# An earlier start for the expert stage's second half: four blocks fewer before it, other gather due times, and two input loads on another DMA queue

## The reference, cut to what matters

```python
s1, s2 = q1 @ keys1.T, q2 @ keys2.T            # per head, 128 keys each
v1, i1 = top_k(s1, 16); v2, i2 = top_k(s2, 16)
top_v, top_i = top_k(v1[:, None] + v2[None, :], 16)
ids = e1 * 128 + e2; w = softmax(top_v)         # 8 heads x 16 = 128 picks a token
act = einsum('td,tkd->tk', h, u[ids])
out = einsum('tk,tkd->td', w * gelu(act), v[ids])
```

## Time and profile before

| | |
|---|---|
| median of 3 runs | 1645.26 us |
| profiled execution | 1646.56 us |
| its span in the trace | 1644.8 us |
| TensorE busy | 1535.6 us (93%) |
| VectorE busy | 1245.2 us (76%) |
| ScalarE busy | 575.4 us (35%) |
| GpSimd busy | 412.1 us (25%) |
| mean DMA rate | 263 GB/s |

### The profile page before, as it was taken

One profiled execution on the slowest core, in us unless ns is written; L12 is line 12 of the kernel. 1 busy time (PEld: TensorE's weight loads), 2 busy tenths in 40 slices (PEclk: granted clock), 3 DMA queues, 4 the chain that ended last, 5 costly groups with the idle time before them and its releaser, 6 DMA issues.

```text
span 1644.8 us, 21695 instructions
## 1 busy us (share of the span) xinstructions
PE 1535.6 (93%) x8105; PEld 1342.2 (82%) x8105; DVE 1245.2 (76%) x2343; ACT 575.4 (35%) x842; POOL 412.1 (25%) x330
## 2 busy tenths in 40 slices
PE   6899987859999899899999999969999999999997
PEld 1588877647899788899999998968888888888886
DVE  1775256764779999799999975638888888888884
ACT  3322150342223233344444443323433333333332
POOL 0000000010026677733222223314222222222211
PEclk9899897989999999999999999989999999999999
DMA  8386110311336777779999999979999998999971
GB/s 351 127 308 243 39 51 1 103 39 52 128 105 205 236 259 259 242 252 356 369 369 367 365 365 395 352 288 400 401 338 367 359 348 331 350 376 340 350 272 65
DMA packets 147829, 432.61 MB, mean 263 GB/s; under 512 B 13232, under 2 KB 46384, under 8 KB 144560
## 3 DMA queue, kind: packets, MB, share of 16 engines
q1 hardware_dynamic: 76896, 221.28, 36.8%
q0 software_dynamic: 36864, 134.23, 23.1%
q10 hardware_dynamic: 34000, 76.29, 12.2%
HBM read 377.22 MB, written 54.53 MB: 263 GB/s over the span
## 4 chain that ended last, share of the span: by engine, by line
PE 60%; DVE 12%; DMA 2%; issue 1%; ACT 1%; POOL 0%; ACTq 0%
PE ps L1547 19%; PE ps L1548 19%; PE ps L1549 19%; PE ps L1872 3%; DVE rows L1355 2%; DVE ps L1387 1%; DMA blk_raw<-u_t 1%; DMA g_dram<-g_buf 1%; DVE ps L1391 1%; DVE picks L1393 1%; PE ps L1824 1%; DVE tv L1322 1%; DVE tv L1325 1%; DVE ti L1323 1%; DVE ti L1326 1%
## 5 line engine op out<-in xcount | busy, mean ns | idle before, releaser
L1547 PE MATMUL ps<-hT_hi,ws_hi 128*128 128x384 f32 (+1 forms) x1184 | 417.0, 352 | 34.6 <-POOL ws_lo L562 16.7
L1548 PE MATMUL ps<-hT_lo,ws_hi 128*128 128x384 f32 (+1 forms) x1184 | 409.1, 346 | 0.0
L1549 PE MATMUL ps<-hT_hi,ws_lo 128*128 128x384 f32 (+1 forms) x1184 | 408.8, 345 | 0.0
L1547 PE MATMUL ps<-vs_hi,coef_hi 128*128 128x512 f32 x768 | 299.8, 390 | 3.9 <-DVE coef_lo L1521 3.9
L1548 PE MATMUL ps<-vs_lo,coef_hi 128*128 128x512 f32 x768 | 299.7, 390 | 0.0
L1549 PE MATMUL ps<-vs_hi,coef_lo 128*128 128x512 f32 x768 | 299.6, 390 | 0.0
L1547 PEld LDWEIGHTS ps<-hT_hi,ws_hi 128*128 128x128 f32 x1184 | 225.6, 191 | 47.4 <-issue 19.5
L824 ACT ACTIVATE ws_hi<-blk_raw 128x1024 fp32r<-128x1024 f32 x128 | 135.7, 1060 | 349.1 <-PE ps L1549 326.4
L888 ACT ACTIVATE vs_hi<-blk_raw 128x1024 fp32r<-128x1024 f32 x128 | 135.7, 1060 | 311.7 <-PE ps L1549 302.5
L570 POOL DMA_INDIRECT rows<-v_nat,ids x128 | 137.5, 1074 | 396.1 <-DVE ps L1472 374.0
L1518 DVE TENSOR_TENSOR vs_lo<-blk_raw,vs_hi 128x1024 fp32r<-128x1024 f32 x128 | 156.8, 1225 | 102.3 <-ACT vs_hi L888 101.5
(11 more groups left out here) (284 smaller groups left out, 1855.1 us busy)
## 6 DMA issues: line engine op xcount, KB each, us to landing
blk_raw<-u_t SPq DMA_DIRECT2D x128, 512.0 KB
blk_raw<-v_nat SPq DMA_DIRECT2D x128, 512.0 KB
g_dram<-g_buf ACTq DMA_DIRECT2D x128, 192.0 KB
w_dram<-w_stage SPq DMA_DIRECT2D x48, 512.0 KB
grp_g<-g_dram ACTq DMA_DIRECT2D x16, 1536.0 KB
grp_w<-w_dram ACTq DMA_DIRECT2D x16, 1536.0 KB
part_w<-w_ada SPq DMA_DIRECT2D x32, 512.0 KB, 6.0
raw<-w_in SPq DMA_DIRECT2D x20, 512.0 KB, 7.0
```

The lines of the kernel that those rows point to most:

```text
L1547: pe.matmul(o, lh, rh, start=start, stop=False, skip_group_check=True)
L1548: pe.matmul(o, lh, rl, start=False, stop=False, skip_group_check=True)
L1549: return pe.matmul(o, ll, rh, start=False, stop=stop, skip_group_check=True)
```

## The change

`PART_A` goes from 46 to 42, which moves `EXP_AT` from 42 to 38, `REST_DVE` from 48 to 44 and `PART_END` from 100 to 96. `EARLY_ROWS` goes from 6 to 4. A block without a spread takes no row (before three), and the blocks from 96 to 121 take the difference: 52 rows in 26 blocks, before 32 rows in 22. The blocks 122 to 127 take two v rows each, before one. The gathers' due times start earlier: the first at block 7 instead of 10, and row k of the search is expected to be used at block 10 + 23k/20 instead of 14 + 9k/8. At the start, `xs` and `cx` are loaded by ScalarE's queue behind `colp`, instead of by SP's ahead of `ada_w`.

```diff
-PART_A = 46
+PART_A = 42
 EXP_AT = PART_A - 4
 REST_DVE = PART_A + 2
-EARLY_ROWS = 6
+EARLY_ROWS = 4
@@ act_rows
     if b < PART_END:
-        return 3 if spreads_after(b) is None else 1
-    late = PICKS - EARLY_BLOCKS * SEARCH_ROWS - EARLY_ROWS - STEPS - 3 * (PART_END - PART_A - STEPS)
+        return 0 if spreads_after(b) is None else 1
+    late = PICKS - EARLY_BLOCKS * SEARCH_ROWS - EARLY_ROWS - STEPS
@@ mix_rows
     if b < EB:
-        return 1
-    late = PICKS - (EB - MIX_FROM)
+        return 2
+    late = PICKS - 2 * (EB - MIX_FROM)
@@ gathers_at
-    used = [14 + 9 * k // 8 for k in range(EARLY_BLOCKS * SEARCH_ROWS)] + [PART_A - 3] * EARLY_ROWS
+    used = [10 + 23 * k // 20 for k in range(EARLY_BLOCKS * SEARCH_ROWS)] + [PART_A - 3] * EARLY_ROWS
-    first = [used[k - G_RING] + 2 if k >= G_RING else 10 + k for k in range(PICKS)]
+    first = [used[k - G_RING] + 2 if k >= G_RING else 7 + k for k in range(PICKS)]
@@ SP's queue
-            sp.dma_start(xs[:], x.rearrange("(b p) d -> p b d", p=P)).then_inc(x_in, 16)
-            sp.dma_start(cx[:], ctxt.rearrange("(b p) d -> p b d", p=P)).then_inc(cx_in, 16)
@@ ScalarE's queue
             act.dma_start(colp[:], cols).then_inc(cols_in, 16)
+            act.dma_start(xs[:], x.rearrange("(b p) d -> p b d", p=P)).then_inc(x_in, 16)
+            act.dma_start(cx[:], ctxt.rearrange("(b p) d -> p b d", p=P)).then_inc(cx_in, 16)
             act.dma_start(ident[:], ident_in).then_inc(ident_ld, 16)
```

## The result

The changed kernel took 1662.08 us (median of 4 runs, 1658.83 to 1663.66), the kernel before 1644.28 beside it (4 runs, 1642.31 to 1646.56): ratio 1.0105 [1.0084, 1.0127], slower. The forecast was 1648.0 and its range ended at 1659. The profiled execution of after took 1661.87 us with a span of 1660.1, 15.3 us more than before; by the medians it is 17.8, since the profiled execution of before was its longest run. I account for the 15.3. The first gelu, ScalarE's in block 0, marks the start of the expert stage.

What follows compares the result with a forecast made beforehand. Bounds: TensorE in both long stages, VectorE's search between 549 and 697 us, the DMA briefly behind the spreads. Terms -4.3 - 11.5 + 16.6 + 1.9 = +2.7 us gave 1648.0 us on the median, range 1637 to 1659.

Steps and rivals of the forecast that it cites:

- The start: Program start: with tokens and ada_w in two queues, the transposes begin at 26.8 instead of 31.12 us, -4.3 us.
- two queues with work each get half: Loads at the start: each of the two queues gets 209 of the 418 GB/s.
- My bound of 0: Program start: the worst case of the -4.3 us term, late tokens eating the whole gain.
- Rival C: Program start: the queues serve the tokens first, giving -1 instead of -4.3 us, time 1651.3; chance 0.07.
- The spreads' begin: End of the search: the part with spreads begins at 685.3 instead of 696.83 us, -11.5 us.
- the stop of 10 us: Search: TensorE stands still in front of block 13 for about 10 us, waiting for row 0.
- Rival D: Search: earlier due times bring no row earlier, -7.6 instead of -11.5 us, time 1651.9; chance 0.10.
- Four blocks: Behind the spreads' begin: 86 blocks left instead of 82, at 4.16 us each, +16.6 us.
- DMA in blocks 96 to 121: End of the u half: two rows a block at 418 GB/s make a block 4.235 us, +1.9 us over 26 blocks.
- waiting beside the stores: Behind the last spread: eight stores delay one block by 7.00 us, taken as unchanged.
- rival B: End of the u half: gathered rows come late and hold up VectorE, +8.6 instead of +1.9 us, time 1654.7; chance 0.16.
- Blocks 122 to 127: End of the u half: six added v rows, 3.1 MB, taken as 0, with 7.5 us more if nothing hides them.

Runs made afterwards that it cites:

- e1: The kernel before with only the loads of xs and cx moved to ScalarE's queue behind colp: 1651.03 us against 1642.77, ratio 1.0059.
- e3: The changed kernel with one v row instead of two in each of blocks 122 to 127: 1657.67 us, ratio 1.009 to the kernel before.
- e8: The kernel before with the first ada_w piece ahead of xs and cx in SP's queue: 1642.38 us, ratio 0.9987.
- e4: The changed kernel with the u and v rows per block of the kernel before: 1655.23 us, ratio 1.0076 to the kernel before.
- e7: The changed kernel with the v half's first group load in ten pieces in blocks 110 to 120: 1654.52 us, ratio 1.0062 to the kernel before.

## Why the prediction was wrong

**The start, -4.3: wrong in sign, +5.5 at the transposes and +2.9 at the first gelu.** The step that failed is "two queues with work each get half". Measured, `ada_w` got 2.4 times the bytes of `xs`, and with pieces of equal size 1.2 times; so `xs` was used at 21.23 us instead of the 13.7 of the sum, and `cx` at 28.31 instead of 18.6. My bound of 0 was wrong as well. I had taken it that late tokens could eat no more than the gain, but TensorE had nothing else to do while they were late, and it came back at half the clock. Rival C named the right doubt, with a price of -1, and its argument that tokens go first was the wrong way round. The Trainium skill's rule that issuing from several engines saves only the time to issue ("DMA: Bandwidth & Descriptors", "Issuing engines are not separate DMA queues") would have given the same -1. That is nearer to the measured loss than my -4.3, but e1, with its loss of 8 us in the medians, shows that a second queue also changes who is served.

**The spreads' begin, -11.5: right, -10.8.** Row 23 gained 4.1 (3.9 forecast) from the two short L1395. TensorE continued behind the copies of the picks and not behind GpSimd, as forecast. Two details differ: the stop of 10 us came in two parts, and the wait behind the transposes' start was 2.9 us, not 3.6. Rival D, by which VectorE gains nothing, is out. What I didn't see is that the same rows also price the due times alone (+6.5): that the term is negative at all is owed to the four blocks moved behind it.

**Four blocks, +16.6: right** as far as it can be told apart from the next term; the part with spreads is right, 40.1 us per eight blocks.

**DMA in blocks 96 to 121, +1.9: right in sum, +2.3, by luck.** The rate was 417 GB/s as forecast, but the spacing behind the stores was 4.18 us and not 4.235, so the slower pace, over all 26 blocks in my sum, gave only 0.3 us in the last 16. The rest is more waiting beside the stores, which I had taken as a constant, and which the experiment with the old rows shows not to be one. One sign that I had named for rival B came true: VectorE waited 13.2 us for gathered rows, with next to no effect on TensorE.

**Blocks 122 to 127: taken as 0, measured +5.2.** I had the six added v rows as an upper bound of 7.5 us, and took the value at its lower end, as if TensorE's work would hide them. e3 prices them at 3.9 us. I did not read the wait of 11.05 us that stood in exactly these blocks before: a stretch that already waits for the DMA hides nothing. This is akin to rival B's mechanism, full DMA and late loads, in another place and with another chain (group load, gelu stores, gelu, TensorE instead of rows, subtraction, TensorE).

With the two failed terms at their measured sizes the sum is +2.9 - 11.5 + 16.6 + 1.9 + 5.2 = +15.1, against 15.3 in the traces. The medians differ by 17.8 us, and the 2.5 between the two figures lie within what single executions differ.

## What to carry to other kernels

Before moving a load to a second queue, compare the sizes of the descriptors (the contiguous pieces, here rows, that a DMA is made of) with those it will run beside. Here the queue with the larger ones got the larger share, and what was needed first was in the other. A term hidden "behind TensorE" must be looked up in the stretch where it lands, for a wait that is already there. When an in-order queue carries both blocks for the bound engine and fetches for a chain that waits for nobody, give each fetch the time at which the trace shows its consumer, no earlier.

## What the hardware showed that I had not expected

- Two queues with loads under way at 423 to 424 GB/s in all (8 to 28 us of the changed kernel) shared the bytes 2.4 to 1 with rows of 8 KB against 4 KB, and 1.2 to 1 with 4 KB each.
- After a stop of 11.55 us TensorE ran at a granted clock of 0.50 in the window from 28 to 40 us, and e8's at 0.58 from 16 to 24 behind a stop of 6.81. Both held up a chain that had nothing else to run.
- Issuing can take long: the fourth small load behind `xs` and `cx` took ScalarE 2.38 us (1.97 to 2.30 in e1, e3, e4 and e7), where the others took 0.41 to 0.78. With the two issues more it put off the first table load, and `csil` to 8.09 (5.50 before). With `ada_w` in halves the same issue took 0.51, and SP's sixteen took 17.10 us in all; what decides it is not shown.
- One core alone drew 417 GB/s for 72 us in the u half, and as many as 428 in four us of e8's start.
